# Differential attention in a two-block kernel: 128-row score passes, one scaling ratio, and a new order on two engines

## What is computed

```python
logits = einsum('bqhmd,bshmd->bhmqs', qi, k) * scale
logits = logits - slopes[h] * dist
logits = where(dist >= 0, logits, -inf)
p = softmax(logits, axis=-1)
attn = p[:, :, 0] - lam * p[:, :, 1]
out = einsum('bhqs,bshe->bqhe', attn, v)
...
attn = rmsnorm(out, subln_w) * (1.0 - lambda_init)      # eps 1e-5, over the 128 values of a head
y_a = attn.reshape(b, s, DA_WIDTH) * silu(g_a)
```

## Time and profile before

| what | value |
|---|---|
| median of 3 runs | 2057.66 us (2057.37 to 2057.93) |
| the profiled execution | 2083.68 us, its span 2081.9 us |
| mean granted TensorE clock | 0.911 of full speed |
| busy: PE, DVE, ACT, POOL | 1836.1, 1011.6, 775.6, 70.0 us |
| chain that ended last | PE 79%, DVE 12%, issue 4%, ACT 3% |

### The profile page before, as it was taken

One profiled execution on the slowest core, in us unless ns is written; L12 is line 12 of the kernel. 1 busy time (PEld: TensorE's weight loads), 2 busy tenths in 40 slices (PEclk: granted clock), 3 DMA queues, 4 the chain that ended last, 5 costly groups with the idle time before them and its releaser, 6 DMA issues.

```text
span 2081.9 us, 23598 instructions
## 1 busy us (share of the span) xinstructions
PE 1836.1 (88%) x8490; PEld 1468.6 (71%) x8490; DVE 1011.6 (49%) x1635; ACT 775.6 (37%) x1358; POOL 70.0 (3%) x90
## 2 busy tenths in 40 slices
PE   5897699999989799998988978988996997798987
PEld 4787577777767688886867875657884666677966
DVE  5234466666444565563234335565364234535654
ACT  3122144444332455552132125444154352315651
POOL 0000012000000000000000000000000000000001
PEclk8789599999999899999999998787997898898998
DMA  7321001111234133332222230010321011111111
GB/s 182 90 61 41 1 11 61 61 56 50 93 101 131 51 101 101 92 87 80 96 75 81 86 101 1 21 41 21 116 62 61 21 41 47 61 61 41 42 41 41
DMA packets 155316, 135.74 MB, mean 65 GB/s; under 512 B 9616, under 2 KB 150800, under 8 KB 155104
## 3 DMA queue, kind: packets, MB, share of 16 engines
q1 hardware_dynamic: 150656, 121.35, 19.7%
q0 software_dynamic: 3136, 10.78, 1.5%
q10 hardware_dynamic: 1440, 2.50, 0.4%
HBM read 127.28 MB, written 7.34 MB: 65 GB/s over the span
## 4 chain that ended last, share of the span: by engine, by line
PE 79%; DVE 12%; issue 4%; ACT 3%; DMA 1%; SPq 1%; DVEq 0%; POOL 0%; ACTq 0%
PE bank L294 18%; PE bank L296 18%; PE bank L295 18%; PE bank L1018 3%; PE bank L989 2%; PE bank L1002 2%; DVE wlo L287 1%; PE bank L883 1%; ACT whi L280 1%; PE bank L476 1%; PE bank L2484 1%; PE bank L2120 1%; DVE ssn L443 1%; PE bank L1668 1%; PE bank L1666 1%
## 5 line engine op out<-in xcount | busy, mean ns | idle before, releaser
L294 PE MATMUL bank<-hh,whi 128*128 128x512 f32 (+2 forms) x1104 | 452.5, 410 | 37.0 <-DVE hl L415 20.1
L295 PE MATMUL bank<-hl,whi 128*128 128x512 f32 (+2 forms) x1104 | 441.7, 400 | 0.0
L296 PE MATMUL bank<-hh,wlo 128*128 128x512 f32 (+2 forms) x1104 | 441.0, 399 | 0.0
L280 ACT ACTIVATE whi<-wraw 128x2048 fp32r<-128x2048 f32 x112 | 213.9, 1911 | 396.0 <-PE bank L296 392.6
L287 DVE TENSOR_TENSOR wlo<-wraw,whi 128x2048 fp32r<-128x2048 f32 x112 | 256.3, 2289 | 197.8 <-ACT whi L280 196.4
L294 PEld LDWEIGHTS bank<-hh,whi 128*128 128x128 f32 (+2 forms) x1104 | 212.4, 192 | 98.9 <-issue 25.7
L296 PEld LDWEIGHTS bank<-hh,wlo 128*128 128x128 f32 (+2 forms) x1104 | 212.6, 193 | 48.6
L295 PEld LDWEIGHTS bank<-hl,whi 128*128 128x128 f32 (+2 forms) x1104 | 213.3, 193 | 43.6 <-issue 1.7
L1042 DVE COPY pt<-bank 128x128 f32<-128x128 f32 (+2 forms) x96 | 42.6, 469 | 104.4 <-PE bank L1002 104.4
L294 PE MATMUL bank<-ah,whi 128*128 128x512 f32 x192 | 77.1, 401 | 12.0 <-DVE al L2619 8.5
L1052 ACT ACTIVATE pr<-bank,nm 128x128 f32<-128x128 f32 (+3 forms) x128 | 66.2, 529 | 46.5 <-DVE nm L1113 46.4
(11 more groups left out here) (360 smaller groups left out, 3116.4 us busy)
## 6 DMA issues: line engine op xcount, KB each, us to landing
wraw<-in_w_in_a_dram SPq DMA_DIRECT2D x52, 512.0 KB, 4.5
wraw<-in_w_up_dram SPq DMA_DIRECT2D x42, 512.0 KB, 4.8
wraw<-in_w_in_dram SPq DMA_DIRECT2D x34, 512.0 KB, 4.7
wraw<-in_w_in_c_dram SPq DMA_DIRECT2D x18, 512.0 KB, 4.3
wraw<-in_w_down_dram SPq DMA_DIRECT2D x16, 512.0 KB, 4.3
wraw<-in_w_out_a_dram SPq DMA_DIRECT2D x16, 512.0 KB, 4.3
aside<-stage POOLq DMA_DIRECT2D x20, 256.0 KB, 2.3
w<-in_cmp_w_dram SPq DMA_DIRECT2D x4, 1024.0 KB, 12.6
```

Source lines behind the costliest of these rows:

```text
L280: act.activation(whi[:, p], wraw[:, p], ACT.Copy).then_inc(w_hi_done, 1)
L294: pe.matmul(out, ws[0], hs[0], start=first, stop=False)
L295: pe.matmul(out, ws[0], hs[1], start=False, stop=False)
L296: return pe.matmul(out, ws[1], hs[0], start=False, stop=last)
```

## The change

It has six parts.

1. The middle score pass contracts 128 rows: the low keys of a map stand in the rows of the high queries, and the same low keys once more in the other 64 rows, opposite the low queries. They go to a tile of their own, `kl2`, so that both key passes have the same shape and all three passes take 128 rows. The two halves in the map's own rows are made by GpSimd (`diff_low_own`), the crossed halves by VectorE.
2. The two maps are combined as p0 + p1 * r, r = -lambda * sum0 / sum1, in one pass; p0 is no longer divided by its sum. The norm over a head takes the scale out again, with its epsilon multiplied by the square of sum0; all the sums are kept for that.
3. VectorE scales step u-1 ahead of the maxima of step u.
4. The low parts are made in steps i=0 and 1; ScalarE makes the first three high parts of head h+2 in step i=3 of head h, and the other three in step i=0 of head h+1. Its copy of the gate bank goes ahead of the exponentials of step i=0.
5. The distances, the lambda product and all parts of head 0 are made during `diff_values`.
6. In the tail VectorE squares sum0, and forms the epsilon term and the bank's sums in one more step ahead of the square root.

```diff
+    kl2 = at("kl2", Y, [2, 2, S], F32R)
+    sga = at("sga", Y + 48 * K, [KT, S])
+    def diff_high(act, h, step):
+        if step == 0:
+            for m in range(2):
+                rows = slice(HD * m, HD * m + HD)
+                act.activation(qs2[rows, h % 2, m, :], q2[rows, h, :], ACT.Copy)
+            act.activation(kh2[0:HD, h % 2, 0, :], k2[0:HD, h, :], ACT.Copy).then_inc(q_hi, 1)
+        else:
...
+    def diff_low(dve, h, step):
+        if step == 0:
+            dve.wait_ge(q_hi, NH // 2 + h + 1)
...
+        else:
+            dve.wait_ge(k_hi, h + 1)
+            for m in range(2):
+                rows, other = slice(HD * m, HD * m + HD), slice(HD - HD * m, P - HD * m)
+                dve.tensor_tensor(kl2[other, h % 2, m, :], k2[rows, h, :], kh2[rows, h % 2, m, :].bitcast(F32),
+                                  ALU.subtract).then_inc(k_lo, 1)
+    def diff_low_own(pool, h):
+        pool.wait_ge(k_hi, h + 1)
+        for m in range(2):
+            rows = slice(HD * m, HD * m + HD)
+            ins = pool.tensor_tensor(kl2[rows, h % 2, m, :], k2[rows, h, :], kh2[rows, h % 2, m, :].bitcast(F32),
+                                     ALU.subtract)
+        ins.then_inc(k_own, 1)
     def diff_values():
...
         @block.scalar
         def _(act):
+            act.wait_ge(drained, m0)
+            act.dma_start(distf[:, :], con[:, CCOL["dist"]:CCOL["dist"] + S]).then_inc(got_con, 16)
+            diff_high(act, 0, 0)
+            diff_high(act, 0, 1)
+            act.wait_ge(got_con, CON2)
+            act.activation(dist[:, :], distf[:, :], ACT.Copy).then_inc(d_ready, 1)
             with act.Fori(0, 2) as i:
...
             def scores(u):
...
                     pe.wait_ge(q_lo, QB + h + 1)
+                    pe.wait_ge(k_lo, 2 * h + 2)
+                    pe.wait_ge(k_own, h + 1)
...
-                    pe.matmul(out, qs2[:, h % 2, m, P * i:P * i + P], kh2[:, h % 2, m, 0:wd], start=True, stop=False)
-                    pe.matmul(out, qs2[rows, h % 2, m, P * i:P * i + P], k2r[rows, h, 0:wd], start=False, stop=False)
+                    for part in (kh2, kl2):
+                        pe.matmul(out, qs2[:, h % 2, m, P * i:P * i + P], part[:, h % 2, m, 0:wd], start=part is kh2,
+                                  stop=False)
...
             for u in range(STEPS + 3):
                 h, i = u // TT, u % TT
+                if 0 < u <= STEPS and i == 0:
+                    act.wait_ge(tiles, 2 * n0 + h)
+                    act.activation(sga[:, h - 1, :], bank[7][:, :], ACT.Copy).then_inc(drained, 1)
...
+                    if (i == 3 or u == 0) and h + 2 - (u == 0) < DA_H:
+                        high_parts(h + 2 - (u == 0), 0)
+                    if i == 0 and h + 1 < DA_H:
+                        high_parts(h + 1, 1)
+                        diag(h + 1)
...
+            def weighed(v):
+                h, i = v // TT, v % TT
+                wd = P * (i + 1)
+                dve.wait_ge(p2_exp, 2 * v + 2)
+                if v:
+                    dve.wait_ge(p2_done, v)
+                r = rs2[:, v % 2, 0:1]
+                dch(dve, dve.reciprocal(r, sm2[:, 1, i, h:h + 1]))
+                dch(dve, dve.tensor_scalar(r, r, sm2[:, 0, i, h:h + 1], nlam[:, 2:3], ALU.mult, ALU.mult))
+                a, b = pr2[:, v % 2, 0, 0:wd], pr2[:, v % 2, 1, 0:wd]
+                dve.scalar_tensor_tensor(out=a, in0=b, scalar=r, in1=a, op0=ALU.mult, op1=ALU.add).then_inc(p2_done, 1)
             for u in range(STEPS + 2):
+                h, i = u // TT, u % TT
+                if 1 <= u <= STEPS:
+                    weighed(u - 1)
                 if u < STEPS:
+                    maxima(u)
...
-                    if h + 1 < DA_H and i in (2, 3):
-                        low_parts(h + 1, "q" if i == 2 else "k")
+                    if h + 1 < DA_H and i < 2:
+                        diff_low(dve, h + 1, i)
...
-            act.activation(rta[:, :, :], bank[4][:, 0:TT * DA_H].rearrange("p (t h) -> p t h", t=TT), ACT.Sqrt,
-                           bias=eps[:, 1:2], scale=1.0 / P).then_inc(a_inv, 1)
+            act.wait_ge(a_inv, 1)
+            act.activation(rta[:, :, :], rta[:, :, :], ACT.Sqrt, scale=1.0 / P).then_inc(a_inv, 1)
...
+            dch(dve, dve.tensor_tensor(es2[:, :, :], sm2[:, 0, :, :], sm2[:, 0, :, :], ALU.mult))
+            dve.wait_ge(a_used, DA_H)
+            dve.scalar_tensor_tensor(out=rta[:, :, :], in0=es2[:, :, :], scalar=P * EPS2,
+                                     in1=bank[4][:, 0:TT * DA_H].rearrange("p (t h) -> p t h", t=TT), op0=ALU.mult,
+                                     op1=ALU.add).then_inc(a_inv, 1)
```

More of the change, by code:

```diff
@@ L1575, in two_blocks @@
     rra = at("rra", S2 + 288, [TT, DA_H])
+    es2 = at("es2", S2 + 416, [TT, DA_H])
     distf = at("distf", SC_AT, [S])
@@ L1606, in _ @@
                         mm.then_inc(tiles, 1)
+            pe.wait_ge(l_step, 1)
+            pe.matmul(bank[4][:, 0:2], ones[:, :], lprod[:, :], start=True, stop=True).then_inc(l_step, 1)
+        @block.gpsimd
+        def _(pool):
+            diff_low_own(pool, 0)
         @block.scalar
         def _(act):
+            act.wait_ge(drained, m0)
[4 more added lines that the diff above has]
+            act.activation(dist[:, :], distf[:, :], ACT.Copy).then_inc(d_ready, 1)
             with act.Fori(0, 2) as i:
@@ L1615, in _ @@
         def _(dve):
+            lamc = pcol("lam", 0, n=4).rearrange("p (a b) -> p a b", b=2)
+            dve.tensor_tensor(lprod[:, :], lamc[:, :, 0], lamc[:, :, 1], ALU.mult).then_inc(l_step, 1)
+            diff_low(dve, 0, 0)
+            diff_low(dve, 0, 1)
             with dve.Fori(0, 2) as i:
@@ L1647, in _ @@
         def _(pe):
[L1648 to L1651, removed]
             pe.wait_ge(d_ready, 1)
@@ L1712, in _ @@
             values(DA_H - 1)
+        @block.gpsimd
+        def _(pool):
+            for h in range(1, DA_H):
+                diff_low_own(pool, h)
         def turned(eng, u, signal, copy):
@@ L1734, in diag @@
                 act.activation(dg2[:, h % 2, :], ident[:, :], ACT.Copy, scale=sl[h]).then_inc(dg_done, 1)
[L1736 to L1753 removed]
+            def high_parts(h, step):
+                if h >= 2 and step == 0:
+                    act.wait_ge(s2_done, 8 * (h - 1))
+                diff_high(act, h, step)
             def out_head(h):
@@ L1809, in low_parts, with maxima @@
-            def low_parts(h, what):
-                dve.wait_ge(q_hi, QB + h + 1)
-                low(h, 0, what)
-                ins = low(h, 1, what)
-                if what == "k":
-                    ins.then_inc(q_lo, 1)
-            low_parts(0, "q")
-            low_parts(0, "k")
+            dch(dve, dve.scalar_tensor_tensor(out=nlam[:, 2:3], in0=nlam[:, 1:2], scalar=-LAMBDA_INIT,
+                                              in1=nlam[:, 0:1], op0=ALU.add, op1=ALU.subtract))
+            def maxima(u):
+                wd = P * (u % TT + 1)
+                for m in range(2):
+                    dve.wait_ge(s2_done, 2 * u + m + 1)
+                    if u >= 2:
+                        dve.wait_ge(p2_exp, 2 * (u - 2) + m + 1)
+                    dve.tensor_reduce(nm2[:, u % 2, m:m + 1], bank[2 * (u % 2) + m][:, 0:wd], AX, ALU.max,
+                                      negate=True).then_inc(s2_max, 1)
```

98 lines of the change are left out of this document (23 added, 75 removed).

## The result

The changed kernel took 2039.85 us, the median of four runs (2034.83 to 2041.09); beside it the kernel before took 2057.8 (2057.37 to 2068.28, four runs). The ratio is 0.988, with a 95% interval of 0.985 to 0.991: faster by 18 us, where 56 were forecast, and outside the forecast range. Two more sets of six runs, made with the experiments, gave 2032.84 and 2024.65, with ratios 0.983 (0.978 to 0.988) and 0.982 (0.977 to 0.987). The profiled execution took 2034.83 us, its span is 2033.0. I begin with the busy time by stretch, in the columns of the earlier trace rows: the values projection, the attention, what follows to the next norm, and the rest.

A forecast was written before the change was run, and what follows sets the result against it. In the attention no engine is saturated: TensorE waits on VectorE's queue and loses clock. Entry 8.8, heads 34, clock 14, less 0.3 give 56.5 us on the profile, 56 on the median: 2057.7 to 2002 us, range 1988 to 2026.

The forecast's parts named there:

- part 3: VectorE's queue in the attention: scaling goes first, one pass gone; TensorE waits 1.6 us a head in place of 3.4.
- part 5: GpSimd's two subtractions a head in the attention: 1.0 to 1.3 us each, costing 0.2 us a head.
- part 4: Clock in the attention: 6 us lost at the low level in place of 20, saving 14 us; ends 0 and 17.
- Part 1: Entry to the attention: head 0's preparation moves to the values projection, first scores 8.8 us earlier; ends 7 and 9.5.
- Part 2: Score passes in the attention: middle pass over 128 rows instead of 64 saves 2.8 to 3.0 us a head.
- the tail: End of the attention: one more VectorE step between the row sums and the root adds about 0.3 us.
- Rival C: Attention: middle score pass saves nothing or the queues bind, heads save 12 to 20 us; 2020 to 2032 us, chance 0.12.

The follow-up runs named there:

- b_entry: Kernel before with only the new entry (head 0's split, distances and lambda product moved into the values projection): 2057.38 us, ratio 0.997 to before.
- b0: Kernel before, run again unedited with its own profile: 2062.53 us, ratio 1.000.
- a0: Changed kernel, run again unedited: 2032.84 us, ratio 0.983 to the kernel before.
- a_rep: Changed kernel, run once more unedited in a later batch: 2024.65 us, ratio 0.982 to the kernel before.
- a_late2: Changed kernel with GpSimd's subtractions held until the head's second combining pass is done, second run of this edit: 2011.33 us, ratio 0.979 to before.
- b_fill: Kernel before with five filler matmuls in each wait of the state-space scan: 2084.84 us, ratio 1.007 to before.

## Why the prediction was wrong

The sign, the order of the parts and the shape of the stage were right; the sum of 56 was too large. The steps that failed are the waits in part 3 and what GpSimd does to them in part 5, the size of the clock term in part 4, and the silence about the part behind the attention. By the prediction's own steps:

- **Part 1, the entry: right.** 8.8 forecast, 8.9 in the profile, 8.7 in b_entry.
- **Part 2, the score passes: right as a duration; as a term it holds only with part 3 beside it.** 1.08 to 0.69 us for three passes of 512 columns is what was forecast; for 128 columns it is 0.62 to about 0.35, where 0.39 was forecast. But undone alone part 2 is worth 5 us of stage, not 22, since TensorE's waits on VectorE shrink as its passes grow.
- **Part 3, VectorE's queue: the bound, and half the saving.** Undone, the pass is worth 11 us of stage and the order 13. But the step "1.6 us a head in place of 3.4", 13 us in seven heads, failed. In before, b0 and b_entry TensorE idles 17.5, 19.6 and 19.0 us in the stage on VectorE's queue, in after, a0 and a_rep 13.8, 13.6 and 15.1. With the 0.16 us that a matmul's record runs on at each wait, that is 2.8 us a head before and 2.0 after: about 6 us saved. The waits view of b0 shows which waits they were:

```profile
PE bank L1676 <- DVE pr L1838: 14.0, 17, 1.4
...
PE bank L1665 <- issue: 5.6, 7, 0.8
```

The waits ahead of the next head's scores (the second line) are gone; those on the combining pass are as long as before, 13.6 to 15.1. The 3.4 came from one head of one trace, where the mean of the stage was 2.8. The 1.6 is reached in a_late2, with GpSimd held: 10.3 us of idle time in 13 waits, 1.55 a head. In the mean of these three traces each, with the lost clock taken off, the stage went from 146.6 to 119.6: **27 us where parts 2 and 3 had 34**, near the lower end given, 25. The estimate is rough: for the kernel before alone the three traces give 143.6 to 148.7.
- **Part 4, the clock: 12 for 14 in the mean** (20.8 lost in three traces of before's attention, 9.1 in three of after's), but 22 between the two profiled executions and 5 against b0. The mean leans on the first trace, which is longer than all 76 other runs; without it the term is 7 (16.5 lost in the mean of b0 and b_entry). It is the term with the largest spread, and it was sized on an execution that was 26 us above the median, by which all terms were then scaled alike. Its stage was 173 us, the others of that attention 163, 166 and 167 (b_fill): 10 of the 22 us by which it exceeds b0 sat in this very stage.
- **Part 5, GpSimd: named, and undersized.** 0.2 us a head forecast; holding it is worth 9.6 us in the stage, about 4 of them without the clock, 0.6 a head, and TensorE's waits agree (14.2 to 10.3 us). The step that failed is "most of it where PE has values to do": VectorE lost 1.4 us a head, in two or three heads of seven on the combining pass that TensorE waits for, and the waits behind the weight split, forecast at 0.9 us, were 1.8 to 1.9 until GpSimd was held. The end given for the subtractions (1 us a head) would have come closer.
- **Not in the forecast: what lies behind.** 0.3 us was forecast for the tail. With a scan of 101 us in both, it is 364.0 us (a_rep) against 362.1 (b0) to the next norm. With the long scan it is 382. Nine of the changed kernel's 16 runs are in the upper group; at 18.5 us each that is 10 us of the mean. The kernel before spreads as widely (2055.6 to 2077.5 us), but in no clear groups, and none of its traces without fillers has a scan over 107 us, so what share of its mean comes from the scan isn't known. Whether the change makes the long form more frequent is **open**: nine of 16 are too few to tell.

In the pair of traces with equal scans (b0, a_rep) the gain is 38 us: against the forecast the stage lacks 14 of 48 (8 of them in the clock term), the part behind takes 2, and 2 are noise in other parts. The means of all runs are 34 us apart; that the scan takes the other 4 is likely but not shown. The recorded 18 is the 34 with the luck of four runs each: before's three at 2057.4 to 2057.9 are near the lowest of its 76 others, after's four are all in the upper group. Rival C's range (2020 to 2032), with its reason that VectorE's queue binds, came nearest, and the mean of the 16 runs, 2031.8, lies in it; the range should have reached further up, since a part of the kernel that no edit touches moves by 18 us between executions.

## What to carry to other kernels

When two savings act on engines that wait for each other, a term has no price of its own: cost each with the other undone and with it done, and forecast the chain. Count the waits over the whole stage, not in one head. Before work goes to GpSimd, look which VectorE instruction with two on-chip operands will stand beside it; one wait that moves it beside reads of PSUM was worth as much as a removed pass. And take a stage's length from more than one execution before a term is sized on it.

## What the hardware showed that was not expected

- The same scan, instruction for instruction, took 101 or 119 us in two executions of one kernel, at mean granted clocks of 0.93 and 0.77 (a_rep and after; from the last value matmul to the next norm 364.0 and 382.8 us).
- Two waits of 1.87 and 1.89 us within 5 us were followed by 4 us at a clock of 0.57; the 14 us of the head ahead, without such waits, stand at 1.00. In the same stage the clock also fell behind single waits of 2.14 us (0.54 in 1243 to 1246) and 1.86 us (0.50 in 1315 to 1318).
- Filler matmuls in a wait made the kernel before 0.7% slower, with a scan of 119.1 us in the trace, TensorE recorded busy in 118.5 of 120 us of it and the clock at 0.79.
- A pass over 64 rows slows both neighbours: 1.09 us for three passes of 512 columns in place of 0.69 (0.33, 0.42 and 0.34 where each was 0.23).
